# Output map of the first mixer: two token passes with 512 moving columns in place of four column blocks of 256

## What is computed

```
y_x = concat([fourier_mix(u_x), a_x]) @ w_out     # (256, 1024) @ (1024, 1024), the same for the context
x   = x + mx[2] * rms_norm(y_x, norm_w[i, 1])      # post norm with its gate row
hx  = modulate(rms_norm(x, norm_w[i, 2]), mx[3], mx[4])
fx  = swiglu(hx, ffn_gu_w, ffn_down_w)             # up and gate (1024, 5632), down (2816, 1024)
```

## Time and profile before

| | us |
|---|---|
| median of three runs | 2195.5 |
| lowest and highest | 2193.95 and 2196.22 |
| profiled execution, its time | 2193.92 |
| span of that execution in the trace | 2192.1 |
| PE busy in the span | 2005.0 (91%) |
| DVE busy | 1508.1 |
| ACT busy | 1268.4 |

### The profile page before, as it was taken

The page is one execution under the profiler, slowest core; times in us unless marked ns, Lnnn a source line. Parts: engine busy times, 40 slices in busy tenths (PEclk is TensorE's granted clock), DMA queues, the critical chain, the costliest instruction groups (busy, mean ns, idle before and its releaser), DMA issues. The chain is left out here.

```text
span 2192.1 us, 31819 instructions
## 1 busy us (share of the span) xinstructions
PE 2005.0 (91%) x11771; PEld 1673.7 (76%) x11772; DVE 1508.1 (69%) x1838; ACT 1268.4 (58%) x1706; POOL 94.5 (4%) x81
## 2 busy tenths in 40 slices
PE   4989879999997898997768999999999999999997
PEld 3967878888876676776666888888788888878885
DVE  2155342223466666876756989898989989898997
ACT  4234353222456345445355877778778787878775
POOL 0000000000000022232300000000000000000000
PEclk8999989999999899998888999999999999999998
DMA  8359512332444222220064999999999999999994
GB/s 313 116 183 383 205 39 84 100 99 99 158 169 143 78 65 71 58 69 28 20 212 159 370 348 352 341 367 337 372 362 336 355 338 358 351 350 343 365 364 153
DMA packets 249655, 493.97 MB, mean 225 GB/s; under 512 B 10108, under 2 KB 74956, under 8 KB 249548
## 3 DMA queue, kind: packets, MB, share of 16 engines
q1 hardware_dynamic: 249547, 492.50, 62.9%
HBM read 491.42 MB, written 1.05 MB: 225 GB/s over the span
## 5 line engine op out<-in xcount | busy, mean ns | idle before, releaser
L1782 DVE TENSOR_TENSOR lo<-raw,hi 128x1024 fp32r<-128x1024 f32 x836 | 1012.4, 1232 | 369.6 <-ACT hi L1293 281.6
L1310 ACT ACTIVATE hi<-raw 128x1024 fp32r<-128x1024 f32 x672 | 711.8, 1064 | 195.7 <-PE bank L698 195.4
L696 PE MATMUL bank<-hi,xh_t 128*128 128x512 f32 (+1 forms) x1312 | 474.1, 361 | 16.9 <-DVE lo L1782 11.8
L698 PE MATMUL bank<-hi,xl_t 128*128 128x512 f32 (+1 forms) x1312 | 469.4, 358 | 0.0
L697 PE MATMUL bank<-lo,xh_t 128*128 128x512 f32 (+1 forms) x1312 | 469.3, 358 | 0.0
L1293 ACT ACTIVATE hi<-raw 128x1024 fp32r<-128x1024 f32 x164 | 172.2, 1064 | 319.2 <-PE bank L897 174.0
L696 PEld LDWEIGHTS bank<-hi,xh_t 128*128 128x128 f32 x1312 | 250.9, 191 | 56.5 <-issue 15.7
L697 PEld LDWEIGHTS bank<-lo,xh_t 128*128 128x128 f32 x1312 | 251.0, 191 | 36.6 <-issue 1.9
L698 PEld LDWEIGHTS bank<-hi,xl_t 128*128 128x128 f32 x1312 | 250.7, 191 | 35.3
L696 PE MATMUL bank<-hi,hth 128*128 128x512 f32 x624 | 251.3, 403 | 0.8 <-DVE lo L1782 0.2
L698 PE MATMUL bank<-hi,htl 128*128 128x512 f32 x624 | 243.8, 391 | 0.0
(11 more groups left out here) (278 smaller groups left out, 2166.8 us busy)
## 6 DMA issues: line engine op xcount, KB each, us to landing
raw<-in_moe_gu_w_dram SPq DMA_DIRECT2D x224, 1024.0 KB, 6.9
raw<-in_moe_down_w_dram SPq DMA_DIRECT2D x112, 1024.0 KB, 6.2
raw<-in_ada_w_dram SPq DMA_DIRECT2D x24, 2048.0 KB, 10.5
raw<-in_ffn_gu_w_dram SPq DMA_DIRECT2D x22, 1024.0 KB, 5.1
raw<-in_ffn_down_w_dram SPq DMA_DIRECT2D x22, 1024.0 KB, 4.9
raw<-in_ssm_in_w_dram SPq DMA_DIRECT2D x16, 1024.0 KB, 5.4
raw<-in_ssm_out_w_dram SPq DMA_DIRECT2D x8, 1024.0 KB, 5.4
raw<-in_mix_in_w_dram SPq DMA_DIRECT2D x5, 1024.0 KB, 12.4
```

The source lines that it names most:

```text
L696: mm(o, a_hi, w_hi, start=first, stop=False, **kw)
L698: return mm(o, a_lo, w_hi, start=False, stop=last, **kw)
L1310: A_(hi[:, p % SPL, :], raw[:, u, (p % 2) * PIECE:(p % 2 + 1) * PIECE], ACT.Copy).then_inc(m_hi, 1)
L1782: TT(lo[:, p % SPL, :], raw[:, u, h * PIECE:(h + 1) * PIECE], hi[:, p % SPL, :].bitcast(F32), ALU.subtract).then_inc(done, 1)
```

## The change

The output map now takes the weights twice. A unit is a half of the input rows (512) by a half of the output columns (512), so that four units make the matrix, and eight are loaded: one set for the latent blocks, one for the context blocks. `mix_out(i)`, i = 0 to 15, uses one piece (256 inputs, 512 output columns) for two token blocks: 12 matmuls with 512 moving columns. Pass 0 writes banks 0 to 3, pass 1 banks 4 to 7. All four gate rows, the post norm of blocks 0 and 1 and the pre-norms 4 and 5 are now placed between the pieces of the pass. What followed the map for the context blocks stays behind it. PSUM banks of the feed-forward stage are exchanged (0 to 3 with 4 to 7) to fit.

```
-S_FFN = S_MIXOUT + U_MIXOUT
+S_FFN = S_MIXOUT + 2 * U_MIXOUT
...
 SP
-            for i in range(U_MIXOUT):
-                load_cols(S_MIXOUT + i, A["mix_out_w"][0], i * UCOL)
+            for i in range(2 * U_MIXOUT):
+                half, kh = divmod(i % U_MIXOUT, 2)
+                u = unit_of_split(S_MIXOUT + i)
+                load(u, "split", S_MIXOUT + i, rawv(u, 4),
+                     wcols(A["mix_out_w"][0][kh * 4 * P:(kh + 1) * 4 * P, :], half * 512, 512))
...
 PE
-            linear(S_MIXOUT, LIN_MIXOUT)
...
-            pe.wait_ge(mod_ready, 8)
-            pe.wait_ge(lin_evac, LIN_SSMOUT)
-            for r in range(2):
-                grow_(r)
-            for n in (4, 5):
-                norm_t(n)
-            pe.wait_ge(grow_ready, 2)
+            def mix_out(i):
+
+                ps, r = divmod(i, N_MIXOUT // 2)
+                half, q = divmod(r, 4)
+                p = P_MIXOUT + i
+                pe.wait_ge(lo_ready, p + 1)
+                if i == N_MIXOUT // 2:
+                    pe.wait_ge(grow_ready, 4)
+                for b2 in range(2):
+                    a = (2 * ps + b2) * P
+                    for t in range(2):
+                        k = 2 * q + t
+                        m = tok3(bank[4 * ps + 2 * b2 + half][:, :], xh[:, k, a:a + P], xl[:, k, a:a + P],
+                                 *wpart(p, t, 512), first=(k == 0), last=(k == KC - 1))
+                m.then_inc(piece_used, 1)
+
+            for i in range(N_MIXOUT):
+                mix_out(i)
+                if i == 1:
+                    pe.wait_ge(mod_ready, 8)
+                    grow_(0)
+                    grow_(1)
+                if i == 5:
+                    pe.wait_ge(grow_ready, 2)
+                    grow_(2)
+                    grow_(3)
+                if i in (12, 13):
+                    norm_t(i - 8)
             pe.wait_ge(xsplit_done, 6)
...
             up(0, 0, 0, 2 * P)
+            pe.wait_ge(lin_evac, LIN_SSMOUT)
             norm_t(6)
             norm_t(7)
             up(0, 1, 0, 2 * P)
             pe.wait_ge(xsplit_done, 8)
             up(0, 0, 2 * P, 4 * P)
-            grow_(2)
-            grow_(3)
             up(0, 1, 2 * P, 4 * P)
-            pe.wait_ge(grow_ready, 4)
...
 ACT
-            lin_out(S_MIXOUT, LIN_MIXOUT, y)
+            def mix_evac(ps, half):
+
+                act.wait_ge(piece_used, P_MIXOUT + 8 * ps + 4 * half + 4)
+                for b2 in range(2):
+                    A_(y[:, 2 * ps + b2, half * 512:(half + 1) * 512], bank[4 * ps + 2 * b2 + half][:, :], ACT.Copy
+                       ).then_inc(lin_evac, 1)
+
+            for i in range(N_MIXOUT):
+                hi_to(P_MIXOUT + i + 1 + SPL)
+                if i == 2:
+                    grow_out(0)
+                if i == 3:
+                    grow_out(1)
+                    mix_evac(0, 0)
+                if i in (5, 6):
+                    grow_out(i - 3)
+                if i == 7:
+                    mix_evac(0, 1)
+                    act.wait_ge(lin_evac, LIN_MIXOUT + 4)
+                if i in (7, 8):
+                    post_a(i - 7)
+                if i in (10, 11):
+                    norm_a(i - 6)
+                if i == 11:
+                    mix_evac(1, 0)
+                if i in (13, 14):
+                    norm_b(i - 9)
+                if i == 15:
+                    mix_evac(1, 1)
             act.wait_ge(lin_evac, LIN_SSMOUT)
-            post_a(0)
-            grow_out(0)
-            post_a(1)
-            norm_a(4)
-            norm_a(5)
-            grow_out(1)
             post_a(2)
-            norm_b(4)
-            norm_b(5)
             post_a(3)
...
 DVE
-            for u in range(U_MIXOUT):
-                lo_to(2 * (S_MIXOUT + u) + 2 + SPL)
-            post(0)
-            post(1)
-            norm_a(4)
-            norm_a(5)
+            for i in range(N_MIXOUT):
+                lo_to(P_MIXOUT + i + 1 + SPL)
+                if i in (8, 9):
+                    post(i - 8)
+                if i in (10, 11):
+                    norm_a(i - 6)
+                if i in (13, 14):
+                    norm_b(i - 9)
             post(2)
-            norm_b(4)
-            norm_b(5)
             post(3)
```

More of the change, by code:

```diff
@@ L400, in grow_bank, with norm_bank @@
         def grow_bank(r, k):
-            return bank[(0 if r in (2, 3) else 4) + 2 * (r % 2) + k]
+            return bank[4 + 2 * (r % 2) + k]
+        def norm_bank(n, k):
+            return bank[(4 if 6 <= n < 10 else 0) + 2 * (n % 2) + k // 4][:, (k % 4) * P:(k % 4 + 1) * P]
         def grow_of(n):
@@ L456, in build @@
         LIN_MIXOUT = U_MIXIN * NBLK
-        LIN_SSMOUT = LIN_MIXOUT + U_MIXOUT * NBLK
+        LIN_SSMOUT = LIN_MIXOUT + 2 * NBLK
+        P_MIXOUT, N_MIXOUT = 2 * S_MIXOUT, 4 * U_MIXOUT
         RT_N = 1
@@ L486, in ffn_bank @@
         def ffn_bank(j, i):
-            return bank[4 * ((j + 1) % 2) + i]
+            return bank[4 * (j % 2) + i]
         block = es.enter_context(nc.Block())
@@ L739, in norm_t, with mix_in @@
                 for k in range(KC):
-                    m = pe.transpose(bank[2 * (n % 2) + k // 4][:, (k % 4) * P:(k % 4 + 1) * P],
-                                     xn_of(n)[:, k * P:(k + 1) * P], ident)
+                    m = pe.transpose(norm_bank(n, k), xn_of(n)[:, k * P:(k + 1) * P], ident)
                 m.then_inc(xt_done, 1)
-            def linear(s0, lin0):
-                for u in range(U_MIXIN if s0 == S_MIXIN else U_MIXOUT):
+            def mix_in():
+                for u in range(U_MIXIN):
                     for h in range(2):
-                        p = 2 * (s0 + u) + h
+                        p = 2 * (S_MIXIN + u) + h
                         pe.wait_ge(lo_ready, p + 1)
@@ L751, in linear @@
                             if h == 0 and u >= 2:
-                                pe.wait_ge(lin_evac, lin0 + (u - 2) * NBLK + b + 1)
+                                pe.wait_ge(lin_evac, (u - 2) * NBLK + b + 1)
                             for t in range(4):
@@ L772, in _ @@
             pe.wait_ge(ada_done, ADA_FIRST)
-            linear(S_MIXIN, 0)
+            mix_in()
             pe.wait_ge(ld_first, 16)
@@ L910, in down @@
                     for half in range(2):
-                        m = tok3(bank[4 * ps + 2 * b + half][:, :], fth[:, q % 4, b * P:(b + 1) * P],
+                        m = tok3(bank[4 * (1 - ps) + 2 * b + half][:, :], fth[:, q % 4, b * P:(b + 1) * P],
                                  ftl[:, q % 4, b * P:(b + 1) * P], *wpart(p, 0, 1024, half * 512, 512),
@@ L1354, in norm_b @@
                 for k in range(KC):
-                    i = A_(t32_of(n)[:, k * P:(k + 1) * P], bank[2 * (n % 2) + k // 4][:, (k % 4) * P:(k % 4 + 1) * P],
+                    i = A_(t32_of(n)[:, k * P:(k + 1) * P], norm_bank(n, k),
                            ACT.Identity, scale=a_[:, k:k + 1], bias=b_[:, k:k + 1])
@@ L1376, in _ @@
             hi_to(SPL)
[L1378 to L1385, removed]
             def lin_in():
@@ L1483, in y_out @@
                 for half in range(2):
-                    A_(y[:, 2 * ps, half * 512:(half + 1) * 512], bank[4 * ps + half][:, :], ACT.Copy).then_inc(y_evac, 1)
+                    A_(y[:, 2 * ps, half * 512:(half + 1) * 512], bank[4 * (1 - ps) + half][:, :], ACT.Copy).then_inc(y_evac, 1)
             norm_b(6)
@@ L1496, in _ @@
                     A_(sg[c], ffn_bank(j, c)[:, :], ACT.Silu).then_inc(sil_done, 1)
-                if j == 0:
-                    grow_out(2)
-                    grow_out(3)
                 hi_to(p + 3 + SPL)
@@ L1990, in y_out @@
                 for half in range(2):
-                    dve.tensor_copy(y[:, 2 * ps + 1, half * 512:(half + 1) * 512], bank[4 * ps + 2 + half][:, :]
+                    dve.tensor_copy(y[:, 2 * ps + 1, half * 512:(half + 1) * 512], bank[4 * (1 - ps) + 2 + half][:, :]
                                     ).then_inc(y_evac, 1)
```

## The result

In the first comparison the kernel after took 2177.68 us (median of four runs, 2175.6 to 2177.91), the kernel before 2194.72 (four runs, 2193.21 to 2196.22): a ratio of 0.992 with a 95% interval of 0.9903 to 0.9937, faster by 17.0 us. Over all runs of this study the kernel before has a median of 2193.15 us (58 runs, 2190.92 to 2197.57), the kernel after 2178.2 (18 runs, 2175.6 to 2181.65): 15.0 us, the ratio of these two medians is 0.9932. Later comparisons of the kernel after gave 0.9939 (0.9926 to 0.9953), 0.9935 (0.9921 to 0.9948) and 0.994 (0.9923 to 0.9956). The comparisons ran on different chips; in the four later ones the kernel before had medians of 2192.75, 2193.64, 2193.39 and 2193.03 us.

What follows compares the result with a forecast made beforehand. The prediction took matmul rate in the map, then a 22.8 us hole from an ACT/DVE chain, as the bound. Gains of 2.3 (matmuls) and 11.5 (hole) made 13.8, so 2195.5 became 2181.7 us; range 2178 to 2186, then 2187.

Steps and rivals of the forecast that it cites:

- What bounds the stretch: From map start to feed-forward step j = 1 (104.1 us): matmul rate in the map, then an ACT/DVE chain, not weights.
- The hole: 22.8 us between map and first `up`, PE busy for 7.2; idle time and this work forecast to fall to 11.4.
- Matmuls of the map, 2.3 us: In the output map, 178 matmuls at 0.227 us replace 356 at 0.120: 40.4 us for 42.7.
- The hand schedule: Following PE, ACT and DVE through pass and step j = 0 with trace durations: step j = 1 at 332.0, not 345.8.
- Splits in time: In the map, ACT and DVE split each piece within its 2.7 us of matmuls; no PE wait for `lo`.
- Waits in the pass: PE waits 2.3 us for norm 4, 3.7 before the first `up`, 1.1 for the context blocks' split.
- The clock behind the wait: After the wait before the first `up` the clock is low again; the latent `up` takes 8.4 us as before.
- nothing is won by it: In step j = 0, even with a high clock, the context blocks' chain still ends at 320.4.
- Weights: First feed-forward unit, issued at 284.8, lands at 289.9 just when ACT asks; landing in 11.9 us costs 3.4 to 4.5.
- 2195.5 − 13.8 = 2181.7: Whole kernel: median before, 1.6 us above the profiled execution, less the stretch's gain, gives the forecast median.
- moves as a whole: Everything behind the stretch is bound alike in both kernels and only shifts; 1.5 us either side allowed for later stages.
- The base: Whole kernel before: median of 2195.5 us from which the gain was subtracted.

Runs made afterwards that it cites:

- after_256: Kernel after with each matmul of the map cut in two of 256 columns; median 2179.35 us against 2178.28 for the kernel after in the same comparison.
- a_again: Kernel after repeated with no edit; median 2178.28 us against 2192.75 for the kernel before.
- a_fourth: Kernel after repeated with no edit, a fourth look; 2178.94 us against 2193.39 for the kernel before.
- late_ffn: Kernel after, first feed-forward weights requested only when all sixteen pieces of the map are split; median 2183.34 us, 5.2 us above the kernel after.

## Why the prediction was right, and where it was wrong

- **What bounds the stretch**: right. The hole was a chain over ACT and DVE; moving it into the map removed it, and with the map alone changed it stayed (22.9 us for 22.8).
- **Matmuls of the map, 2.3 us**: right by itself (the stretch 2.7 us shorter with the map alone, 2.3 of it from the matmuls), and right against the estimate of 0.5 us from the Trainium skill (TensorE: Matmul & The Clock Gate, "Wait — 56ns, not 53.3ns?"). As a term of the sum it was put wrongly: in the interleaved pass the same matmuls at 256 columns cost some 0.4 us, where the clock at the start of the map is the same. The hand schedule contained this, since it had waits of 2.3 and 3.7 us that end with ACT and DVE; the sum "2.3 from the matmuls and 11.5 from the hole" read it as additive.
- **Splits in time**: right, no wait for `lo`.
- **Waits in the pass**: 2.3, 3.7 and 1.1 us forecast, 1.96, 3.33 and 1.10 measured. The stretch is 89.7 us over four profiles where the forecast had 90.3, and its gain 13.9 where it had 13.8.
- **The clock behind the wait**: right for the profile after, 5.9 us at 0.50 behind a wait of 3.33, but no rule: behind 3.12 us in `after_256` the clock stayed at 1.00, and the last wait then still ended in its place, so that "nothing is won by it" fits. In `a_again` and `a_fourth` it also fell around norm 4 (0.57 and 0.59 over 4 us), for which the prediction had step 1 two microseconds later; their stretches are still 89.5 us; the clock was low for only 2.9 us at the start of their map, where it was 5.5 and 5.9 in the other two.
- **Weights**: right. They came in time; in `late_ffn` an issue 5.8 us later cost 3.5 us of the stretch, what goes beyond a slack of some 2.4.
- **The step that failed** is the last one, "2195.5 − 13.8 = 2181.7", and what it rests on: that all behind the stretch "is bound in the same way in both, and moves as a whole", with 1.5 us to either side for later stages, nothing at all for what stands ahead of the map, and 1.6 us between profile and median. In the first comparison the profiled execution was forecast at 2180.1 us and took 2177.71: of these 2.4 us, 1.94 lie ahead of the map and 0.5 in the stretch (14.34 for 13.8). The 1.6 us that the median was to lie above the profile were nothing (2177.68). Together this is the miss of 4.0 us; the scan stage had no part in that pair, with 302.9 us in both.
- **Over many runs** the same step fails in two other places. The base, a median of three, was 2.3 us above the median of 58 runs of the same kernel. And the parts outside the stretch do not move as a whole: the map starts between 239.7 and 244.5 us, and the scan stage, where the PE is busy for 265 of 303 us and not without a gap as the prediction has it from 345.9 us on, takes 298.7 to 303.9, 302.8 or 302.9 in every profile before and 4.1 less in three of four after. From 2193.15 the forecast would have been 2179.35; the kernel after measures 2178.2. The scan stage can account for the remaining 1.1 us, but how often the executions without a profile had the short one is not seen, and why the kernel after has it more often stays open.
- **The range** was not added up from its own terms: −1 and −1.5 below, +2.2, +2 and +1.5 above give 2179.2 to 2187.4, where the text says first 2178 to 2186 and then 2178 to 2187. That the measured time lies only 0.3 us outside owes something to this.

## What to carry to other kernels

A step that removes a hole by interleaving is best costed by following each engine's list in order, with durations from the trace: it gave 13.8 us for 13.9. Terms of such a schedule need not add up: faster matmuls worth 2.3 us by themselves were worth some 0.4 us inside a pass that ACT and DVE end. Where a gain is below 1%, the base is the median of many runs, and the range must hold what unchanged stages do by chance or when they are shifted. Compare the changed stretch by itself, and before two profiles of it are compared, read the granted clock in it: an unlike clock at its start hid a cost here.

## What the runs showed of the hardware

Granted clock and time of an unchanged stage can depend on work far ahead of it. The scan stage, made of short bursts of matmuls with waits between, ran at a mean granted clock of 0.94 in 302.8 us or more, and at 0.96 in 298.8, with instruction counts that agree within one or two. It had three courses of the clock, each the same to two decimals of the 20 us slices wherever it came. Five matmuls of 0.227 us each, 370 us ahead of it, went with 303.8 us where 298.8 or 302.9 stood, and 303.7 where 302.8 or 302.9 stood; with ten it was 302.9 (one profile each). The time at which the stage starts does not select the course.

The low clock behind a wait is not certain: after 3.33 us of idle PE 5.9 us ran at 0.50, after 3.12 us in another profile the next 5.8 us ran at 1.00. At the start of the map, always behind a wait of 3.02 us, the clock was low for 2.9 to 6.2 us, depending on the profile.

The fixed part of a matmul was larger than expected: 512 columns took 0.227 us, two times 256 took 0.240. If time is otherwise in proportion to the columns, this makes 13 ns for each matmul in this stream, where every one has a weight load beside it. The Trainium skill (TensorE: Matmul & The Clock Gate, "Wait — 56ns, not 53.3ns?") has about 2.5 ns; the measurement decides.
